# A fourth 64-slot expert in a mixture-of-experts trunk, and full and small experts in turn

## The reference

```python
D_MODEL = 1024; SEQ = 256; N_EXPERTS = 8; TOP_K = 2; EXPERT_FF = 3584

def moe_swiglu(h, w_router, w_gate, w_up, w_down):
    logits = (h @ w_router).astype(jnp.float32)
    top_vals, top_idx = lax.top_k(logits, TOP_K)
    top_w = jax.nn.softmax(top_vals, axis=-1)
    combine = jnp.sum(jax.nn.one_hot(top_idx, N_EXPERTS, dtype=jnp.float32) * top_w[..., None], axis=-2)
    y = jnp.zeros_like(h)
    for e in range(N_EXPERTS):
        y = y + combine[..., e:e + 1] * swiglu(h, w_gate[e], w_up[e], w_down[e])
    return y
```

## Time and profile before

| what | value |
|---|---|
| median of 3 runs (lowest to highest) | 1433.05 us (1431.82 to 1436.28) |
| span of the profiled execution | 1434.6 us |
| mean granted TensorE clock | 0.993 |
| PE busy, DVE busy, ACT busy | 96%, 66%, 56% |
| moved by DMA | 459.17 MB, 320 GB/s over the span |

### The profile page before, as it was taken

How to read it: one execution, slowest core, us unless ns; L and a number is a source line. 1 busy time by engine, 2 the same in 40 slices (tenths; PEclk the granted TensorE clock), 3 DMA queues, 4 the chain that set the end, 5 groups by cost and what they waited for, 6 DMA issues and landing times.

```text
span 1434.6 us, 16889 instructions
## 1 busy us (share of the span) xinstructions
PE 1380.0 (96%) x6602; PEld 1015.1 (71%) x6602; DVE 939.7 (66%) x930; ACT 800.1 (56%) x897; POOL 50.0 (3%) x61
## 2 busy tenths in 40 slices
PE   9999999999999999999979999999988999999986
PEld 7977888888887788884228887886325887887321
DVE  5777755556677768883128888885116888888123
ACT  6566454344565667773137777775216777777212
POOL 1000000000000009200000000000000000000100
PEclk9999999999999999999999999999998999999999
DMA  9933655545653459998999999998999999999996
GB/s 346 380 103 118 205 176 193 189 137 204 195 183 124 177 194 397 410 390 337 421 421 423 421 421 407 391 374 335 422 423 421 421 420 411 391 382 379 374 422 263
DMA packets 96293, 459.17 MB, mean 320 GB/s; under 512 B 7657, under 2 KB 13305, under 8 KB 53201
## 3 DMA queue, kind: packets, MB, share of 16 engines
q1 hardware_dynamic: 91632, 444.57, 79.6%
q10 hardware_dynamic: 3120, 8.67, 1.7%
q0 software_dynamic: 1456, 4.79, 0.8%
HBM read 447.00 MB, written 11.01 MB: 319 GB/s over the span
## 4 chain that ended last, share of the span: by engine, by line
PE 78%; DMA 11%; DVE 5%; ACT 3%; issue 1%; SPq 0%; ACTq 0%; DVEq 0%
PE A L503 15%; PE A L505 15%; PE A L504 15%; PE A L509 6%; PE DN L503 5%; PE DN L505 5%; PE DN L504 5%; DMA raw<-in_moe_w_down 5%; DMA raw_more<-in_moe_w_down 3%; PE DN L509 3%; DVE wlo L477 2%; DMA raw<-in_moe_w_up 2%; ACT whi L470 2%; PE T L2093 1%; DMA xs<-in_x 1%
## 5 line engine op out<-in xcount | busy, mean ns | idle before, releaser
L477 DVE TENSOR_TENSOR wlo<-raw,whi 128x2048 fp32r<-128x2048 f32 (+1 forms) x197 | 441.2, 2242 | 142.1 <-ACT whi L470 141.7
L470 ACT ACTIVATE whi<-raw 128x2048 fp32r<-128x2048 f32 (+1 forms) x197 | 369.4, 1877 | 186.1 <-PE A L505 115.3
L477 DVE TENSOR_TENSOR wlo<-raw_more,whi 128x2048 fp32r<-128x2048 f32 x96 | 219.6, 2289 | 27.4 <-ACT whi L470 27.3
L470 ACT ACTIVATE whi<-raw_more 128x2048 fp32r<-128x2048 f32 x96 | 184.2, 1919 | 78.8 <-PE A L505 40.4
L503 PE MATMUL A<-whi,heTh 128*128 128x512 f32 x560 | 222.1, 397 | 2.0 <-DVE wlo L477 2.0
L505 PE MATMUL A<-whi,heTl 128*128 128x512 f32 x560 | 218.8, 391 | 0.0
L504 PE MATMUL A<-wlo,heTh 128*128 128x512 f32 x560 | 218.6, 390 | 0.0
L503 PE MATMUL A<-whi,hTh 128*128 128x512 f32 (+2 forms) x448 | 174.4, 389 | 1.5 <-DVE wlo L1096 0.7
L505 PE MATMUL A<-whi,hTl 128*128 128x512 f32 (+2 forms) x448 | 169.9, 379 | 0.0
L504 PE MATMUL A<-wlo,hTh 128*128 128x512 f32 (+2 forms) x448 | 169.8, 379 | 0.0
L503 PE MATMUL DN<-whi,aTh 128*128 128x512 f32 x320 | 126.2, 394 | 7.0 <-DVE aTl L1545 7.0
(11 more groups left out here) (347 smaller groups left out, 1782.3 us busy)
## 6 DMA issues: line engine op xcount, KB each, us to landing
raw<-in_moe_w_gate SPq DMA_DIRECT2D x63, 1024.0 KB, 13.6
raw<-in_moe_w_up SPq DMA_DIRECT2D x61, 1024.0 KB, 13.5
raw<-in_moe_w_down SPq DMA_DIRECT2D x60, 1024.0 KB, 12.4
raw_more<-in_moe_w_down SPq DMA_DIRECT2D x52, 1024.0 KB, 15.4
raw_more<-in_moe_w_up SPq DMA_DIRECT2D x51, 1024.0 KB, 13.5
raw_more<-in_moe_w_gate SPq DMA_DIRECT2D x49, 1024.0 KB, 11.2
raw<-in_w_in SPq DMA_DIRECT2D x22, 1024.0 KB, 6.7
raw<-in_dense_w_down SPq DMA_DIRECT2D x11, 1024.0 KB, 4.9
```

The lines of the kernel that those rows point to most:

```text
L470: nc.scalar.activation(split_slot(u, e)[0][:, :n], raw_of(u, e)[:, :n], ACT.Copy).then_inc(hi_done, 1)
L477: nc.vector.tensor_tensor(lo[:, :n], raw_of(u, e)[:, :n], hi[:, :n].bitcast(F32), ALU.subtract).then_inc(lo_done, 1)
```

## The change

Positions 1, 3, 5 and 7 are small in place of 1, 4 and 7, so four ranks (4 to 7) hold 64 slots in place of three, and `RANK_AT` gives full ranks to the even positions and small ranks to the odd ones. Everything else follows from these two tables: `WHOLE`, `LOAD_ORDER` (which swaps two units at each border from a small to a full expert), the buffers, and the rank from which `room` is 64.

```diff
 SMALL = P // 2
-SMALL_AT = (1, 4, 7)
-RANK_AT = (0, 5, 1, 2, 6, 3, 4, 7)
+SMALL_AT = (1, 3, 5, 7)
+RANK_AT = (0, 4, 1, 5, 2, 6, 3, 7)


 WHOLE = [e * EU + i for e in SMALL_AT for i in range(EU)]
```

## The result

The changed kernel takes 2511.26 us (median of 4 runs, 2508.91 to 2514.04) against 1434.06 us for the kernel before (4 runs, 1431.82 to 1436.28). The ratio is 1.7513, with a 95% interval of 1.7486 to 1.754. The forecast was 2521 us, and its range 2455 to 2635.

The account below looks back on a forecast made before the run. Full experts were taken as bound by PE, small ones by DMA. Profiled 1434.6 us - 31.4 (first sweep) + 1116 (eight second-sweep turns) + 3.4 (end) = 2522.6, less 1.5 to the median: 2521 us; range 2455 to 2635.

Parts of the forecast that it names:

- What bounds the kernel: Expert part: full experts bound by PE, small ones by DMA; DMA time lost in second full experts, positions 3 and 6.
- The step on capacity: Routing: rank 4 has 65 tokens for 64 slots, so the flag becomes 1 and a second sweep runs over all eight experts.
- The turn: One expert's turn of the second sweep: 119.8 + 15.7 + 2 + 2 = 139.5 us, eight of them 1116 us.
- the branch: Jump back at each second-sweep turn: instructions must be fetched anew, taken as 2 us a turn.
- the clock: Start of each second-sweep turn: after a 15 us pause PE's first 4 us give half their work, 2 us; between 0 and 5.
- The gain of the first sweep: From 753.0 us on: DMA stays at 421 GB/s, so the first sweep ends 31.4 us earlier.
- A: Rival: rank 4 counts 64 tokens or less on the chip, so no second sweep runs; 1402 us, chance 5%.
- B: Rival: the second sweep's ring of six buffers starves, 5 us a turn more; 2561 us, chance 8%.
- C: Rival: each jump back in the second sweep costs 8.2 us and not 2; 2571 us, chance 12%.
- D: Rival: only the expert that overflows is repeated, one turn of the second sweep; 1544 us, chance 1%.
- E: Rival: the first sweep's gain is eaten and no second sweep runs; 1433 us, chance 1%.
- One sign: Second sweep: PE at full pace in eight stretches of about 120 us, with 15 to 20 us pauses ended by DVE's L477.

Follow-up runs that it names:

- e1: The changed kernel with the flag's threshold 1.5 in place of 0.5, so an excess of one token starts no second sweep; 1410.38 us, ratio 0.9838.
- e6: The changed kernel with the flag's threshold 1.5 and the small experts at positions 1, 4, 5 and 7; 1423.46 us, ratio 0.9928.
- e4: The changed kernel with expert 0 and ranks 5 to 7 small, at positions 0, 2, 5 and 7, and rank 4 full; 1414.42 us, ratio 0.9863.
- e7: As e4, but with the small experts at positions 0, 3, 5 and 7, so the adjacent full experts stand at 1 and 2; 1414.65 us, ratio 0.9867.
- e3: The changed kernel with the second sweep's loop cut to one turn, for expert 1 alone; 1551.83 us, ratio 1.082.
- e5: The changed kernel with 14 products of ones added on PE after the gathering of each second-sweep turn; 2499.96 us, ratio 1.7434.

## Why the prediction was right

**What bounds the kernel** held. DMA's lost time was in the second full expert of a pair, and e1 and e6, which differ in the order alone, show 13.1 us for one such pair. e4 and e7 show the dip of one pair each; in their time it stands against what small expert 0 pays back.

**The step on capacity** carried the result, and held to the token: e1 shows an excess of exactly one. No view of the kernel before has this in it. It came from the ranks, from the rule that expert 0 is not ranked, and from the counts of the reference; the trace only showed that the sweep had not run so far. "The fourth fewest" of all eight has 62 tokens and would have fitted, while the fourth fewest of those that are ranked has 65.

**The turn** was forecast at 139.5 us and measured at 137.6. By its parts at 1535 us:
- copy to first add 2.0 us (forecast 2.0), two adds 1.55 (1.5), second block to the end of its adds 2.75 (2.7);
- choosing and weighing, the branch back in it, 1541.63 to 1543.13 = 1.5 us, forecast 1.8 and 2 for the branch. The branch is the term that was mis-sized: between the last add and the next turn's first copy on DVE lie 0.2 us, and its compare-and-branch, at 1541.4 us, runs while that add is still at work;
- three splits 6.6 (6.9), `heTl` to the first product 0.4 (0.4);
- PE's part, from the first product to the copy: 123.1 us on average of the eight turns, against 119.8 + 0.4 + 2 for the clock. Without the clock it is 120.1, so the products were right, and the clock took 2.9 us a turn and not 2: 2.1 for the fall that was forecast, 0.8 for the second, which I did not foresee. Nor is the pause one of 15 us, as the forecast had it: PE spreads and gathers in it, and its longest idle time there is 3.7 us.

The branch's own records, and the two instruction queues of the changed kernel (eight turns) and then of e3 (one turn):

```profile
L1621 DVEq COMPARE_BRANCH  x8: 50/56/56, 1541.4 to 2503.1; - x8
L2170 PEldq COMPARE_BRANCH  x8: 83/215/232, 1541.8 to 2503.7; - x8
...
q8 instruction: 56, 0.92, 0.1%
q14 instruction: 31, 0.25, 0.0%
...
q8 instruction: 56, 0.92, 0.2%
q14 instruction: 28, 0.23, 0.0%
```

The Trainium skill (Advanced Engine Details and Errata, Control Flow Timing) gives about 108 ns for a compare-and-branch; here it took 56 ns on DVE and 215 ns on PE at the median, and the measurement decides. The Trainium skill's rule that a taken branch out of the fetched window forces a fetch first (Runtime: NRT & Kernel Launch, Instruction fetch mechanics) has no visible price here. Seven more turns brought 3 more packets in the two instruction queues together, fewer than one a turn. So the prediction's step that the instructions must be fetched anew at each jump back does not hold for these loops.

**The gain of the first sweep** was mis-sized: 26.3 us, not 31.4. Two terms were off. I took 2 us from the last landing to the end, but the last loads run out earlier; here DMA is at 351 GB/s in one stretch and idle in the next:

```profile
1383.00:1393.00 10.00, 8.24 (x40) 2.52 (x38) 3.10 (x4) 1.61 (x3) 0.00 (x0) 1.00 0.84 351
1393.00:1397.00 4.00, 2.80 (x13) 0.48 (x8) 0.65 (x1) 0.60 (x1) 0.00 (x0) 1.00 0.03 12
```

That is 10 x (421 - 351) / 421 + 4 = 5.7 us, of which 2 were allowed. And the full experts ran at 417 to 418 GB/s, not at 421, with DMA busy throughout: 0.9 to 1.1 us each, 2.9 us in three. The sum, 6.6 us, more than covers the 5.1 that are missing; 1 GB/s of rounding is 1.5 us in such a sum. A full expert is not slower as such: at position 2 the loss lies in one stretch, 783 to 793 us at 379 GB/s, and in the kernel before, the same stretch has 418. What lowers the rate there stays open.

**The span and the time.** I set the span of the traced execution against the median as if both measured the same. The traced execution of e5 took 2491.94 us with a span of 2490.1, so 1.8 us lie around the span. By that the traced execution of the kernel before was most likely the slowest of the three shown then, 1436.28 us, 3.2 us above their median and not 1.5. The forecast does not depend on it, as it is the median and the differences, 1433.05 + 1088 = 2521 us. But the gain of the first sweep was counted from a slow execution: it is 26.3 us between the traces and 24.4 us between the medians of e1 and the kernel before.

**The rivals.** A (no second sweep) fell by the counts of L2024; no row bears on its "half of all draws". B (six buffers starve) fell: from 1412 to 2500 us no wait of PE, ACT or DVE is ended by a DMA, and units of the `raw` buffers land in 5.1 to 5.4 us at the median of both sweeps (13.6 and less before). C (dear branches) fell by the 0.2 us. D (one turn only) is e3, forecast 1544, measured 1551.8. E did not occur. One sign was named wrongly: what ends PE's wait for the first product of a turn is not `wlo` (L477) but `heTl` (L1525), which DVE makes right after the three splits.

## What to carry to other kernels

Where a kernel holds data-dependent work in fixed room with a fallback, an edit of the room must first be checked against the counts, and the fallback's price put beside the gain: here 26 us against 1101, decided by one token. Read which items are ranked at all before counting "the fourth fewest". And where fixed stages alternate between two limits, the buffers decide: a stage bound by PE costs DMA nothing as long as the stage before has left the buffers empty: 421 GB/s against 380 here.

## What the runs showed of the hardware that was not expected

A loop's branch back cost DVE 0.2 us between two instructions, and its record there is 56 ns. After 3.7 us in which PE stood still, products ran at half clock (0.50, 1.2 GHz), start to start 0.43 us in place of 0.23, for 5 to 6 us in three turns and about 3 in the other five. Near the end of a turn PE waits 1.8 us for `aTl` in every turn:

```profile
PE DN L503 <- DVE aTl L1545: 14.4, 8, 1.8
```

Behind that wait the clock fell in four turns of eight and stayed in four, with the same instructions in the same order. So two executions of one sequence differ by 2 to 3 us a turn, and a gain of that size needs several traces or many runs.
